# Hybrid trunk, bidirectional gated recurrence: queries and keys decayed in place level by level, with equal halves of the projections

## The reference, cut to what matters

```python
def gla_chunk_step(state, q, v, k, g):
    # S_t = diag(exp g_t) S_{t-1} + k_t v_t^T, o_t = S_t^T q_t
    b = jnp.cumsum(g, axis=-2)
    o_inter = jnp.einsum('...td,...de->...te', q * jnp.exp(b), state)
    diff = b[..., :, None, :] - b[..., None, :, :]
    decay = jnp.exp(jnp.where(lower[:, :, None], diff, -jnp.inf))
    scores = jnp.einsum('...td,...sd,...tsd->...ts', q, k, decay)
    o_intra = jnp.einsum('...ts,...se->...te', scores, v)
    state = jnp.exp(b_end)[..., :, None] * state + jnp.einsum('...sd,...se->...de', k * jnp.exp(b_end - b), v)

def hgrn2_mixer(xc, xl, w_in, lb, norm_g, w_out, need_ctx):
    q, i_in, gate, zf = jnp.split(x @ w_in, ...)      # zf: one part for each direction
    log_f = jnp.log(lb + (1.0 - lb) * jax.nn.sigmoid(zf))
    k = (1.0 - lb) * jax.nn.sigmoid(-zf)
    ...                                               # scan forwards and backwards, sum, RMS norm per head
    return (o * jax.nn.silu(gate)) @ w_out
```

## Time and profile before

| what | value |
|---|---|
| three runs | 2220.99, 2226.67, 2232.32 us (median 2226.67) |
| profiled execution, its time | 2220.87 us |
| its span, first to last instruction | 2218.6 us |
| mean granted TensorE clock | 0.954 |
| PE busy | 2011.3 us (91%) |
| PEld busy | 1635.5 us (74%) |
| DVE busy | 1438.1 us (65%) |
| ACT busy | 653.6 us (29%) |
| POOL busy | 411.1 us (19%) |

### The profile page before, as it was taken

How to read it: one execution, slowest core, us unless ns; L and a number is a source line. 1 busy time by engine, 2 the same in 40 slices (tenths; PEclk the granted TensorE clock), 3 DMA queues, 4 the chain that set the end, 5 groups by cost and what they waited for, 6 DMA issues and landing times.

```text
span 2218.6 us, 26397 instructions
## 1 busy us (share of the span) xinstructions
PE 2011.3 (91%) x10776; PEld 1635.5 (74%) x10776; DVE 1438.1 (65%) x2219; ACT 653.6 (29%) x953; POOL 411.1 (19%) x342
## 2 busy tenths in 40 slices
PE   5989889888957889999999999899989879999997
PEld 2878778777846777888888888775565567777775
DVE  4577786796798457753775277475355468568385
ACT  5312212212210233221322123335434433233232
POOL 2031122123163004433553353000000000000000
PEclk8999999999989989999999999988989999999998
DMA  6121212112110113333333332210010022233232
GB/s 253 48 76 58 67 57 77 48 48 77 48 58 29 48 40 104 114 95 96 113 101 99 94 113 91 89 53 6 1 57 1 29 75 84 87 91 91 85 95 95
DMA packets 56856, 165.85 MB, mean 75 GB/s; under 512 B 6176, under 2 KB 6560, under 8 KB 56608
## 3 DMA queue, kind: packets, MB, share of 16 engines
q1 hardware_dynamic: 56736, 164.17, 23.3%
HBM read 162.05 MB, written 2.10 MB: 74 GB/s over the span
## 4 chain that ended last, share of the span: by engine, by line
PE 69%; DVE 18%; DMA 4%; ACT 4%; issue 2%; POOL 2%; SPq 0%; DVEq 0%; POOLq 0%
PE slot L391 17%; PE slot L393 17%; PE slot L392 17%; DVE ACC L1372 6%; DVE WL L1045 3%; PE slot L705 3%; PE MA L510 3%; DMA WR<-in_w 2%; ACT WH L770 2%; POOL ada_low L350 1%; PE slot L696 1%; PE MB L444 1%; PE MB L445 1%; PE MB L489 1%; DVE PS L1241 1%
## 5 line engine op out<-in xcount | busy, mean ns | idle before, releaser
L391 PE MATMUL slot<-HH,WH 128*128 128x256 f32 (+1 forms) x2016 | 720.5, 357 | 43.9 <-DVE ACC L1380 15.6
L392 PE MATMUL slot<-HL,WH 128*128 128x256 f32 (+1 forms) x2016 | 708.6, 351 | 0.0
L393 PE MATMUL slot<-HH,WL 128*128 128x256 f32 (+1 forms) x2016 | 708.0, 351 | 0.0
L391 PEld LDWEIGHTS slot<-HH,WH 128*128 128x128 f32 x2016 | 385.3, 191 | 118.0 <-issue 50.5
L1045 DVE TENSOR_TENSOR WL<-WR,WH 128x1024 fp32r<-128x1024 f32 x204 | 288.6, 1416 | 256.4 <-ACT WH L770 254.9
L392 PEld LDWEIGHTS slot<-HL,WH 128*128 128x128 f32 x2016 | 385.5, 191 | 52.5 <-issue 2.2
L393 PEld LDWEIGHTS slot<-HH,WL 128*128 128x128 f32 x2016 | 384.6, 191 | 51.2
L770 ACT ACTIVATE WH<-WR 128x1024 fp32r<-128x1024 f32 x204 | 215.2, 1056 | 478.9 <-DMA WR<-in_w 478.7
L1372 DVE SCALAR_TENSOR_TENSOR ACC<-UP,cw,ACC 128x512 f32<-128x512 f32 x352 | 293.0, 832 | 8.6
L348 POOL TENSOR_SCALAR ada_high<-ada_raw 128x512 fp32r<-128x512 f32 x160 | 131.7, 823 | 892.1 <-DMA ada_raw<-in_ada 481.6
L350 POOL TENSOR_TENSOR ada_low<-ada_raw,ada_high 128x512 fp32r<-128x512 f32 x160 | 247.9, 1549 | 13.4
(11 more groups left out here) (197 smaller groups left out, 2233.2 us busy)
## 6 DMA issues: line engine op xcount, KB each, us to landing
WR<-in_w SPq DMA_DIRECT2D x204, 512.0 KB, 3.7
ada_raw<-in_ada SPq DMA_DIRECT2D x160, 256.0 KB, 2.6
AD<-in_ada SPq DMA_DIRECT2D x3, 2048.0 KB, 23.1
X<-in_x SPq DMA_DIRECT2D x1, 3072.0 KB, 19.3
AD<-in_ada SPq DMA_DIRECT2D x4, 512.0 KB, 6.9
out<-Y SPq DMA_DIRECT2D x8, 256.0 KB, 2.2
Y<-in_masks SPq DMA_DIRECT2D x1, 512.0 KB, 25.6
rope<-in_rope SPq DMA_DIRECT2D x1, 512.0 KB, 3.5
```

What stands on the lines that cost most here:

```text
L391: mm(SLOT[s][:, po], WH[w % NB][:, k, :], hi[:, k, to], start=(k == 0), stop=False)
L392: mm(SLOT[s][:, po], WH[w % NB][:, k, :], lo[:, k, to], start=False, stop=False)
L393: last = mm(SLOT[s][:, po], WL[w % NB][:, k, :], hi[:, k, to], start=False, stop=(k == kn - 1))
```

## The change

- The running decays of both directions lie in one tile FD (planes FORE and BACK), the keys in KK, the decayed queries in QQ. A pair's total decay is kept in one element of each block (`total`), not in all of them.
- Queries are decayed once in full (`decayed_queries`, 1536 elements wide), and then in each level the half that crosses a pair is multiplied by the other block's total (`merge_queries`, two half-width products, in place). Keys likewise (`merge_keys`). `mix_keys` copies the wanted halves of the two key planes to KL. `merge_totals` updates the totals, two small products.
- PE reads the queries of a level straight from QQ with an access pattern that alternates between the planes every s elements (`of_level`). Since QQ is changed in place, `merge_queries` waits for PE's scores of its level.
- The diagonal becomes the first set of scores (n = -1), on PE between half tiles n=2 and n=3 of its own step, no longer after n=0 of the next. On DVE its take stands behind `head_out`, and level 0's `mix_keys` behind that.
- `finals` goes: after level 6 queries and keys already are what it made. `products`, `double`, TF and TB go too.
- The recurrence's tiles are split into 384 and 384 columns, at PSUM columns 128 to 896.
- The sums of the head norm go to MB instead of MA and wait for both of ACT's output copies; ACT's square goes to RF. Q has one buffer instead of two.

```diff
+HG0, HG1 = 128, 128 + TOK
+HG_HALVES = [(slice(HG0, 512), slice(0, 384)), (slice(512, HG1), slice(384, TOK))]
...
+        def of_level(t, at, tokens, s):
+            whole = t[:, :, :]
+            return bass.AP(whole.tensor, whole.offset + at, [list(whole.ap[0]), [2 * s, tokens // (2 * s)], [TOK + s, 2], [1, s]])
...
             def level_scores(b, n):
-                level.add()
-                pe.wait_ge(level_ready, level.now())
-                if level.some(1):
-                    pe.wait_ge(scores_read, level.now(1))
-                q = QL[n % 2] if n < LEVELS else Q[b]
+                if n != 0:
+                    level.add()
+                    pe.wait_ge(level_ready, level.now())
+                if n >= 0:
+                    mixed.add()
+                    pe.wait_ge(keys_mixed, mixed.now())
+                if scored.some(0):
+                    pe.wait_ge(scores_read, scored.now())
+                scored.add()
                 for c in range(NCH):
                     t = slice(c * P, (c + 1) * P)
-                    last = mm(MA[:, chunk(c)], KL[n % 2][:, t], q[:, t], start=True, stop=True)
+                    if n < 0:
+                        last = mm(MA[:, chunk(c)], KL[1][:, t], Q[:, t], start=True, stop=True)
+                    else:
+                        last = mm(MA[:, chunk(c)], KL[n % 2][:, t], of_level(QQ[b], c * P, P, 2 ** n), start=True, stop=True)
                 last.then_inc(scores_done, 1)
...
             def head_sums():
                 pe.wait_ge(o_squared, head.now())
-                token_sums(O2, 0)
+                pe.wait_ge(o_evac, head.now())
+                token_sums(RF, 0, MB)
...
                 def between(n):
                     if tail and n == 0:
-                        level_scores(1 - b, LEVELS)
                         key_value(1 - b)
                     if tail and n == 1:
                         outputs(1 - b)
-                    if tail and n == 2:
-                        head_sums()
+                    if n == 2:
+                        if tail:
+                            head_sums()
+                        level_scores(b, -1)
...
+            def decayed_queries(b):
+                mark(tt(QQ[b][:, :, :], Q[:, :].unsqueeze(1).to_broadcast([P, 2, TOK]), FD[b][:, :, :], ALU.mult))
+            def merge_keys(b, n):
+                s = 2 ** n
                 settle()
+                keys.add()
+                dve.wait_ge(keys_mixed, keys.now())
+                k, f = KK[b], FD[b]
+                tt(half(k, 0, s, 0), half(k, 0, s, 0), spread_totals(f, FORE, s, 1), ALU.mult)
+                last = tt(half(k, 1, s, 1), half(k, 1, s, 1), spread_totals(f, BACK, s, 0), ALU.mult)
+                last.then_inc(keys_ready, 1)
+            def mix_keys(b, n):
                 s = 2 ** n
+                if n:
+                    dve.wait_ge(keys_ready, keys.now())
+                for plane in range(2):
+                    k = KL[n % 2][:, :].rearrange("p (n two s) -> p n two s", two=2, s=s)[:, :, plane, :]
+                    last = cp(k, half(KK[b], plane, s, plane))
+                last.then_inc(keys_mixed, 1)
+            def merge_queries(b, n, done):
+                s = 2 ** n
+                dve.wait_ge(scores_done, done)
+                q, f = QQ[b], FD[b]
+                tt(half(q, FORE, s, 1), half(q, FORE, s, 1), spread_totals(f, FORE, s, 0), ALU.mult)
+                last = tt(half(q, BACK, s, 0), half(q, BACK, s, 0), spread_totals(f, BACK, s, 1), ALU.mult)
+                if n < LEVELS - 1:
+                    level.add()
+                    last.then_inc(level_ready, 1)
                 else:
+                    last.then_inc(kq_final, 1)
+            def merge_totals(b, n):
...
+                for plane in (FORE, BACK):
+                    mark(tt(total(FD[b], plane, s, 0), total(FD[b], plane, s, 0), total(FD[b], plane, s, 1), ALU.mult))
...
             def head_step(b, parity, h, j0, tail=True, project=True):
                 forget(b, parity, h)
                 first = tile.now()
-                if tail:
-                    take(LEVELS, 0)
-                products(b, 0)
+                decayed_queries(b)
                 if project:
                     split_low(first + 2)
                 if tail:
-                    states()
-                double(b, 0)
-                products(b, 1)
+                    states(1 - b)
+                diagonal(b)
                 if tail:
                     token_rstd(0)
                     head_out(h - 1)
                 head.add()
-                take(0, 1)
...
+                take(LEVELS)
+                mix_keys(b, 0)
+                for n in range(LEVELS):
+                    merge_keys(b, n)
+                    merge_queries(b, n, taken.now() + 1)
+                    take(n)
+                    if n < LEVELS - 1:
+                        mix_keys(b, n + 1)
+                    merge_totals(b, n)
+                    if project and n in (0, 2, 3, 4):
+                        split_low(first + (3 if n == 0 else n + 2))
```

More of the change, by code:

```diff
@@ L522, in key_value @@
                 pe.wait_ge(v_ready, head.now())
-                for src, dst in ((KF, MB), (KB, MA)):
+                for plane, dst in ((0, MB), (1, MA)):
                     if dst is MA:
-                        pe.wait_ge(scores_read, level.now())
+                        pe.wait_ge(scores_read, scored.now())
                     for c in range(NCH):
-                        last = turn(dst[:, chunk(c)], src[b][:, c * P:(c + 1) * P], ident[:, :])
+                        last = turn(dst[:, chunk(c)], KK[b][:, plane, c * P:(c + 1) * P], ident[:, :])
                     last.then_inc(k_turned, 1)
@@ L1229, in double @@
-                settle()
-                mark(tt(halves(CF[b], s, 1), halves(CF[b], s, 1), both(CF[b], s, 0, s - 1), ALU.mult))
-                mark(tt(halves(CB[b], s, 0), halves(CB[b], s, 0), both(CB[b], s, 1, 0), ALU.mult))
-                settle()
-            def take(n, back):
-                dve.wait_ge(scores_done, level.now(back))
-                if level.some(back + 1):
-                    dve.wait_ge(scores_read, level.now(back + 1))
+                settle()
+                keys.add()
@@ new lines, in merge_totals, with take @@
+            def merge_totals(b, n):
+                if n < LEVELS - 1:
+                    dve.wait_ge(level_ready, level.now())
+                else:
+                    dve.wait_ge(kq_final, head.now())
+                s = 2 ** n
+                for plane in (FORE, BACK):
+                    mark(tt(total(FD[b], plane, s, 0), total(FD[b], plane, s, 0), total(FD[b], plane, s, 1), ALU.mult))
+            taken = Tally()
+            def take(n):
+                taken.add()
+                dve.wait_ge(scores_done, taken.now())
+                if taken.some(1):
+                    dve.wait_ge(scores_read, taken.now(1))
@@ L1300, in head_step @@
                 head.add()
-                take(0, 1)
-                if project:
-                    split_low(first + 3)
-                for n in range(2, LEVELS):
-                    double(b, n - 1)
-                    products(b, n)
-                    take(n - 1, 1)
-                    if project and n in (3, 4, 5):
-                        split_low(first + n + 1)
-                diagonal(b)
-                if not project:
-                    take(LEVELS - 1, 1)
-                double(b, LEVELS - 1)
-                finals(b)
-                if project:
-                    take(LEVELS - 1, 1)
+                take(LEVELS)
[4 more added lines that the diff above has]
+                    take(n)
+                    if n < LEVELS - 1:
+                        mix_keys(b, n + 1)
+                    merge_totals(b, n)
+                    if project and n in (0, 2, 3, 4):
+                        split_low(first + (3 if n == 0 else n + 2))
                 rows.add()
@@ L1334, in _ @@
             head_step(1, 0, 7, j0 + 28, project=False)
-            take(LEVELS, 0)
-            states()
+            states(1)
             token_rstd(0)
```

151 lines of the change are left out of this document (60 added, 91 removed).

## The result

The changed kernel takes 2237.84 us (median of 8 runs, 2233.28 to 2239.53), the kernel before 2225.19 (8 runs, 2220.93 to 2232.32). The ratio is 1.0054, interval 1.0038 to 1.0070: slower by half a per cent. Forecast: 2228, range 2200 to 2252. The time lies in the range, between my forecast and rival 2. The outcome that I held likeliest, no change within 0.5% (0.43), is at best just met: the interval runs from 0.38% to 0.70% slower, and for slower by over 0.5% I had put 0.30. The profiled execution took 2233.28 us, its span is 12.9 us longer than that of before.

A forecast was written before the change was run, and what follows sets the result against it. PE's work plus its waits for DVE was taken as the bound. 2220.87 + 12 (full steps) + 0 (first) - 11.4 (last) = 2221.5 us; 5.8 added for a median, rounded up for the operand: 2228, range 2200 to 2252.

The forecast's parts named there:

- rival 2: At level 0, new wait plus strided operand make the kernel slower: 2248 us, or 2258 if two-element blocks pay; chance 0.30.
- Full step: Six full recurrence steps: each goes from 78.6 to 80.6 us, +12 in all, bounds 0 to +22.
- The wait before level 0: PE waits 3.8 us for head output products, diagonal's take and key copies in every step with a tail; before, none.
- Level 4: In a full step, level 4's scores start 1.7 us late because DVE's merges and copies meet POOL.
- level 5: In a full step, PE still waits 4.9 us before level 5's scores, behind the weight split, instead of 6.48.
- The slow clock: PE at half clock behind its waits: 2.0 us a full step, between 0 and 3.6, at 1.85 for each wait.
- The operand: Level 0's queries alternating between two planes: 0 taken, 0 to +1.3 us for each of 8 heads kept in range.
- one of the signs: Forecast is wrong if a set of level 0's scores is longer than other levels' at the same clock; no size given.
- Step 0: First recurrence step, without a tail: own diagonal and later level 3 offset by a shorter level 5 wait; 0, within 2 us.
- Last step: Last recurrence step, through the end of its tail: gains and losses sum to -11.4 us, bounds -19 to -3.
- Level 0 to level 6: Stretch of the last step paced by DVE's loop, copies meeting POOL in three levels: 31.1 us against 35.8, gain 4.7.
- Rival 1: Full steps: DVE's relief counts in full, waits of 1.7 and 4.9 go; 2186 us, half-way 2206; chance of both 0.27.

The follow-up runs named there:

- run 3: Both edits on the changed kernel: diagonal's take and level 0's key copies ahead of the head output, weight load ahead of the second piece pair; 2162.91 us, ratio 0.9736.
- Runs 1: Changed kernel with the diagonal's take and level 0's key copies moved ahead of the head output on DVE; 2203.61 us, 0.9909 of the kernel before.
- run 8: Changed kernel with only level 0's two key copies moved early, the diagonal's take left behind the head output; 2227.65 us, 1.0013 of the kernel before.
- run 2: Changed kernel with the second pair of piece loads behind the next weight tile in SP's queue instead of ahead; 2196.75 us, 0.9890 of the kernel before.
- run 7: Kernel with both edits, level scores reading 128 adjacent query columns instead of strided ones (output not the attention's); 2160.32 us, 0.9710 of the kernel before.
- run 9: Kernel with both edits, POOL's split of seven finished heads held back until DVE's last query merge; 2159.73 us, beside 2163.77 for both edits again.

## Why the forecast came out as it did

**Full step: +12 forecast, +19.1 measured.** The forecast step, 80.6, was work 68.2, waits 10.4 and slow clock 2.0. For the measured step I take the work from run 3, 70.20 less its wait of 0.85, 69.35. Then 81.56 = 69.35 + waits 8.06 (3.51, 0.85, 3.70) + 4.15 for the slow clock. Term by term:
- The wait before level 0, 3.8 forecast, 3.51 measured, of the composition that I gave. Runs 1 and 8 show that it is this order.
- Level 4, 1.7 against 0.85, and level 5, 4.9 against 3.70: too dear. DVE fell by 11 us a step, not 7, and from its weight split to level 5's scores it took 5.8 us, not 7.3 (322.12 - 316.33). The weight's chain set level 5, as forecast: run 2 removed the wait by moving two DMAs.
- **The slow clock, 2.0 against 4.15, is the term that was furthest off.** I charged it to level 5's wait in most steps and to level 0's in some. It followed both, in every full step. My price of 1.85 for one place was near: start to start, level 0 to level 1 took 8.98 us against 6.83 at full clock (+2.15), level 5 to level 6 8.12 against 6.43 in run 2 (+1.7). Counting it once was the error. The two make 3.85 of the 4.15; the rest I can't place.
- The operand, 0 taken, 0.76 measured a head at full clock (run 7), inside the 0 to 1.3 that I kept. Level 0's set took 2.15 in step 0 where the others took 1.50 at the same clock: one of the signs by which I said I would be wrong, and it came. I had argued from DVE's copy of every other element, another engine's reading; it said nothing of PE's. At half clock, as the set ran in most full steps, it costs hardly anything (2.93 against 2.90).

The waits were overpriced by 2.3 and the clock and operand underpriced by 2.9; the work without the operand was 0.4 too low, a difference for which my walk has no term. That the step came out only 1.0 off is luck in part: these errors cancel. The range of 52 us would have held a good deal more.

**Step 0: 0 forecast, -1.3 measured**, within the 2 allowed.

**Last step: -11.4 forecast, -6.8 measured.** PE's timeline there, to be read against the earlier trace rows:

```profile
657.99 1.50 PE L527 MATMUL MA<-QQ,KL 128*128 128x128 f32 x12
...
665.68 1.51 PE L544 MATMUL MB<-ident,KK 128*128 128x128 f32 x6 [5.21 <-DVE Y L1311]
...
674.33 0.49 PE L559 MATMUL MB<-PS,V 128*128 128x128 f32 x2 [2.18 <-DVE SB L1296]
...
727.41 1.58 PE L527 MATMUL MA<-QQ,KL 128*128 128x128 f32 x12 [2.27 <-DVE KL L1243]
...
731.32 0.84 PE L544 MATMUL MB<-ident,KK 128*128 128x128 f32 x6 [1.35 <-issue]
...
745.41 1.73 PE L492 MATMUL MB<-ones,RF 128*128 128x1 f32 x12 [1.78 <-ACT O L881]
```

Level 6 to outputs 16.3 (forecast 16.8, before 25.2). Outputs to level 0, which starts at 693.12: 18.8 (forecast 18.8, before 12.0). Level 6 to the keys' turn 3.9 (forecast 4.1, before 10.0). Two terms were off. Level 0 to level 6 took 34.3, not 31.1 (before 35.8). Level 0 to level 1 alone is 6.76 of it, where I had 4.4 to 4.9: level 0's set ran at half clock behind its wait of 5.11, and DVE's merge had to wait for it (first row). I had no slow clock in this step. And I let only the two copies of a level meet POOL, while the merges or the small products meet it too (the other rows), so level 3 to level 4 took 7.40:

```profile
696.09 0.56 DVE L1253 TENSOR_TENSOR QQ<-QQ,FD 128x384 f32<-128x384 f32 x1 [1.89 <-PE MA L527]
...
709.56 1.65 DVE L1269 TENSOR_TENSOR FD<-FD 128x96 f32<-128x96 f32 x2
...
713.09 1.64 DVE L1254 TENSOR_TENSOR QQ<-QQ,FD 128x384 f32<-128x384 f32 x1
```

And from the turn to the output projection it is 23.2 against 20.3 before, +2.9 where I had +0.8: the sums wait 1.78 for ACT's copy (0.90 before), and half of PE's outputs in front of them and the spread behind them run at half clock (the spread 2.93 against 1.58). None of this was tested by a run of its own.

**The rivals.** Rival 1 was wrong as to this kernel, and right as to what stood in its way: "the weight comes before DVE asks for it" was its condition, and run 2 made it true. Rival 2 named the right place and both its costs. The clock fell at both waits, as it said (4.15 where it had 3.6); the operand cost half of what it assumed at full clock, and next to nothing on top of the slow clock. The total, 10 us above my forecast and 10 below rival 2's, lies midway between them.

## What to carry to other kernels

When a large group of products is taken off a late engine, first see whether it was late for its work or for something that comes by another queue: here 86 us less work bought nothing until one weight load was put ahead of the pieces and one take and two copies ahead of the head output. Walk the new order and ask what now stands between the last release and the first product of the next phase; the take and the copies in the wrong place cost 34 us. Price each wait of PE together with the slow stretch that the trace shows behind waits like it, once for each place: here waits of 3.51 and 3.70 cost 7.2 us and 4.15 of slow clock, one of 6.48 had cost 1.85 of slow clock. The price is a range, not a number: the same wait of 3.51 cost 1.1 to 2.3.

## What the runs showed of the hardware

- A PE operand that alternates every element between two planes 3 KB apart costs 0.65 us for twelve 128-column products at full clock (2.15 against 1.50), in pairs 0.11 (1.61), in blocks of four and more nothing. At half clock the set takes 2.93 with the stride and 2.90 without. The Trainium skill, "SBUF — State Buffer", in its note on cachelines, wants two consecutive accesses in the same 16 bytes for full speed: by it single elements pay and pairs don't. The trace agrees on single elements; pairs pay a little here.
- Behind PE's waits of 3.09 to 6.5 us in the full steps the clock fell to 0.50 for a while; behind those up to 0.9 it stayed at 1.00, and behind 2.58 in run 9 too. What the slow clock costs is not a matter of the wait's length alone. From level 0's scores to level 1's, over the 6.83 of full clock: 1.4 to 2.3 behind 3.51 in the changed kernel, 1.1 to 1.2 behind the same 3.51 in run 2, 0.8 to 1.5 behind 3.09 in run 8.
- Beside POOL a DVE product of two SBUF tiles, 128x384, took 0.96 to 1.65 us where POOL splits pieces (512 wide), and up to 2.15 where it splits heads (768 wide), against 0.55 alone.
- The attention, which no edit touches, took 139.43 us in the profiled execution of run 9 and 132.56 in that of both edits:

```profile
1551.13:1690.56 139.43, 131.83 (x590) 83.13 (x591) 72.29 (x191) 58.93 (x139) 0.00 (x0) 0.89 0.05 16
```

```profile
1557.59:1690.15 132.56, 124.72 (x590) 78.56 (x591) 72.24 (x191) 59.02 (x139) 0.00 (x0) 0.95 0.06 17
```

Same products, granted clock 0.89 and 0.95; over the traces of all runs this stretch takes 132.6 to 139.4. That stretch alone hides run 9's 6.1 us in the span. A few microseconds are to be read where the edit acts, or in medians, not in the span of one profile. What sets the clock's pattern there stays open.
